# Row fetches of the last 128 tokens spread over selection, gates and U tail, and one row addition per V slab with eight landing buffers

## The reference, cut to what matters

```python
q = (xn @ wq)                      # 8 heads, two halves of 128 each
s = q . subkeys                    # 128 scores per half
v1, i1 = top_k(s[..., 0, :], 16); v2, i2 = top_k(s[..., 1, :], 16)
# the 16 best pairs of a head: idx in 0..16383, gate = softmax of their scores
h = einsum('md,med->me', x, u_tab[idx])          # 128 rows of U for each token
y = einsum('me,med->md', gate * gelu(h), v_tab[idx])
```

## Time and profile before

| | |
|---|---|
| median of 3 runs | 4130.0 us (4121.21 to 4146.6) |
| the profiled execution | 4155.08 us, span 4153.2 us |
| granted TensorE clock, mean | 0.918 |
| busy, share of the span | PE 88%, DVE 68%, ACT 35%, POOL 32% |
| moved by DMA | 814.18 MB, 196 GB/s over the span |

### The profile page before, as it was taken

The page is one execution under the profiler, slowest core; times in us unless marked ns, Lnnn a source line. Parts: engine busy times, 40 slices in busy tenths (PEclk is TensorE's granted clock), DMA queues, the critical chain, the costliest instruction groups (busy, mean ns, idle before and its releaser), DMA issues.

```text
span 4153.2 us, 60538 instructions
## 1 busy us (share of the span) xinstructions
PE 3668.9 (88%) x20002; PEld 3437.5 (83%) x20002; DVE 2809.7 (68%) x5900; ACT 1453.1 (35%) x2136; POOL 1335.5 (32%) x1052
## 2 busy tenths in 40 slices
PE   7966689999997998898899666899999979898987
PEld 5855579999997998898777555799999979888887
DVE  6244446889886787777562444478888868777774
ACT  4311123335674332233333111333357643332333
POOL 0000000214775446665000000011247744466650
PEclk9977779999998999999999676899999989999998
DMA  3200014446888999999321000144468889999991
GB/s 128 78 4 1 1 41 144 148 150 216 294 303 309 328 366 335 341 335 339 102 76 66 1 1 0 66 138 151 151 234 300 294 301 353 346 333 328 340 332 68
DMA packets 340506, 814.18 MB, mean 196 GB/s; under 512 B 25328, under 2 KB 189424, under 8 KB 336752
## 3 DMA queue, kind: packets, MB, share of 16 engines
q1 hardware_dynamic: 92592, 339.05, 23.0%
q0 software_dynamic: 73728, 268.47, 17.2%
q10 hardware_dynamic: 174016, 204.50, 14.8%
HBM read 709.16 MB, written 102.76 MB: 195 GB/s over the span
## 4 chain that ended last, share of the span: by engine, by line
PE 60%; DMA 18%; DVE 14%; issue 5%; DVEq 1%; POOL 1%; ACT 1%; ACTq 1%; SPq 0%; POOLq 0%; PEldq 0%
PE bank L368 15%; PE bank L369 14%; PE bank L370 14%; DMA gath<-slabs,rows_of 11%; PE bank L1100 4%; PE bank L938 3%; DMA g_sb<-gates_dram 3%; DMA gath<-u_rows,rows_of 2%; PE bank L391 1%; DVE acc L1656 1%; PE bank L415 1%; DVE wlo L365 1%; DVE act_w L1617 1%; DVE w_lo L1622 1%; PE bank L1020 1%
## 5 line engine op out<-in xcount | busy, mean ns | idle before, releaser
L365 DVE TENSOR_TENSOR wlo<-raw,whi 128x1024 fp32r<-128x1024 f32 x636 | 803.9, 1265 | 473.0 <-ACT whi L358 443.2
L368 PE MATMUL bank<-act_hi,whi 128*128 128x384 f32 (+1 forms) x3008 | 1082.4, 360 | 45.0 <-ACT hst L694 23.4
L369 PE MATMUL bank<-act_lo,whi 128*128 128x384 f32 (+1 forms) x3008 | 1068.3, 355 | 0.0
L370 PE MATMUL bank<-act_hi,wlo 128*128 128x384 f32 (+1 forms) x3008 | 1067.4, 355 | 0.0
L358 ACT ACTIVATE whi<-raw 128x1024 fp32r<-128x1024 f32 x636 | 673.7, 1060 | 522.9 <-PE bank L370 492.1
L368 PE MATMUL bank<-w_hi,whi 128*128 128x384 f32 x2048 | 713.4, 348 | 126.3 <-DVE w_lo L1622 126.0
L506 POOL TENSOR_TENSOR onehot<-onehot,cidx 128x800 f32<-128x800 f32 x56 | 123.9, 2243 | 1868.5 <-DVEq L1508 1868.5
L369 PE MATMUL bank<-w_lo,whi 128*128 128x384 f32 x2048 | 705.5, 344 | 0.0
L370 PE MATMUL bank<-w_hi,wlo 128*128 128x384 f32 x2048 | 704.5, 344 | 0.0
L368 PEld LDWEIGHTS bank<-act_hi,whi 128*128 128x128 f32 x3008 | 571.6, 190 | 92.7 <-ACT hst L694 24.1
L514 POOL DMA_INDIRECT gath<-slabs,rows_of x256 | 540.5, 2111 | 328.7 <-DVE acc L1656 277.6
(11 more groups left out here) (285 smaller groups left out, 3921.4 us busy)
## 6 DMA issues: line engine op xcount, KB each, us to landing
raw<-slabs SPq DMA_DIRECT2D x636, 512.0 KB, 3.7
hidden_dram<-hst ACTq DMA_DIRECT2D x256, 192.0 KB, 3.1
gates_dram<-stage ACTq DMA_DIRECT2D x24, 2048.0 KB, 7.5
h_sb<-hidden_dram ACTq DMA_DIRECT2D x64, 768.0 KB, 7.7
g_sb<-gates_dram ACTq DMA_DIRECT2D x64, 768.0 KB, 17.3
gath<-u_rows,rows_of POOLq DMA_INDIRECT x256, 7.3
gath<-slabs,rows_of POOLq DMA_INDIRECT x256, 8.7
res<-x_t SPq DMA_DIRECT2D x1, 2048.0 KB, 9.2
```

The source lines that it names most:

```text
L365: nc.vector.tensor_tensor(wlo[k][:], raw[k][:], whi[k][:].bitcast(F32), ALU.subtract).then_inc(s_slab_lo, 1)
L368: nc.tensor.matmul(out, a_hi, b_hi, start=first, stop=False)
L369: nc.tensor.matmul(out, a_hi, b_lo, start=False, stop=False)
L370: return nc.tensor.matmul(out, a_lo, b_hi, start=False, stop=last)
```

## The change

Row numbers of U are made head by head (in `sum_experts`), so that fetches can begin in selection. 32 dot products go into selection: five in each of heads 2 to 7, behind `split_lo` number 1, 3, 5, 7 and 8 of the head, and two after head 7. GpSimd issues five fetches after the `onehot` products of each of heads 1 to 6. 72 go into the gates, one in even batches and two in odd ones; 24 into the U tail, two per slab. V keeps one addition per slab, with eight buffers (four of them in memory that the U stage has freed). `x_nat` gets memory of its own and is made at the second slab of selection instead of near its end; the Gelu of the 128 tokens moves into the U tail; the first `load_hg` moves from slab 0 to slab 3 of the tail. Some constants (`dist`) are loaded again in each layer, to free memory. The diff, cut:

```diff
+GV = 8
+DOT_HEAD = 5
+DOT_SEL = 32
+DOT_LOOP = 12
+DOT_GATE = DOT_LOOP * N_BATCH // 8
+DOT_TAIL = P - DOT_SEL - DOT_GATE
+P_XNAT = 1
+X_TOK = 14
+DOT_AT = (1, 3, 5, 7, 8)
@@ SyncE
+                sp.dma_start(dist[:], consts_d[:, C_DIST:NCONST]).then_inc(S["dist_loaded"], 16)
@@ GpSimd
+                def gather(n):
+                    if n >= GR:
+                        pool.wait_ge(S["gath_used"], n - GR + 1)
+                    if n % TOPK == 0:
+                        pool.wait_ge(S["rows_ready"], n // TOPK + 1)
...
+                def gather_v(n):
+                    if n >= GV:
+                        pool.wait_ge(S["gath_used"], P + n - GV + 1)
+                    elif n >= GR:
+                        pool.wait_ge(s_used, S_V)
+                    else:
+                        pool.wait_ge(S["gath_used"], P - GR + n + 1)
...
                 for hd in range(PH - 1):
                     pool.wait_ge(S["places_ready"], hd + 1)
                     for t in range(NT):
                         rows = onehot[:, t * TOPK:(t + 1) * TOPK, :]
                         nc.gpsimd.tensor_tensor(rows, rows, cidx[:, t, :].unsqueeze(1).to_broadcast([P, TOPK, NC]),
                                                 ALU.mult).then_inc(S["picks_ready"], 1)
+                    if hd >= 1:
+                        for n in range(DOT_HEAD * (hd - 1), DOT_HEAD * hd):
+                            gather(n)
+                for n in range(DOT_HEAD * (PH - 2), DOT_SEL + GR - 1):
                     gather(n)
...
                     last.then_inc(S["hot1_ready"], 1)
-                    gather(b + GR - 1)
+                    for n in range(DOT_LOOP * b // 8, DOT_LOOP * (b + 1) // 8):
+                        gather(n + DOT_SEL + GR - 1)
@@ ScalarE, U tail
                     if x == 0:
+                        act.wait_ge(S["gm_ready"], 2 * TD // 8 + 4)
+                        act.dma_start(p_sb[:], p_t[layer]).then_inc(S["p_loaded"], 16)
+                    if x == 3:
                         act.wait_ge(S["stored_a"], TD // TG // 2 * 16 + 1)
                         act.wait_ge(S["stored_b"], TD // TG // 2 * 16 + 1)
...
                         load_hg(0, 0)
                         load_hg(1, 1)
...
+                    if x == X_TOK:
+                        act.wait_ge(S["gath_used"], P)
+                        nc.scalar.activation(w_tok, h_tok, ACT.Gelu).then_inc(S["tok_gelu"], 1)
@@ VectorE, selection
                 def sum_experts(hd):
                     step(V.tensor_reduce(expert[:, :, hd, :], picks, AX_X, ALU.add))
                     settle()
+                    V.tensor_scalar(rows_u[:, hd * TOPK:(hd + 1) * TOPK], expert[:, NTD, hd, :],
+                                    par[:, Q_ROWS:Q_ROWS + 1], None, ALU.add).then_inc(S["rows_ready"], 1)
...
                         for part in parts:
                             select(hd, part)
+                        if hd >= 2 and k in DOT_AT:
+                            if hd == 2 and k == DOT_AT[0]:
+                                dve.wait_ge(S["xnat_copied"], 2)
+                            n = DOT_HEAD * (hd - 2) + DOT_AT.index(k)
+                            dot(n, n % GR)
+                for n in range(DOT_HEAD * (PH - 2), DOT_SEL):
+                    dot(n, n % GR)
@@ VectorE, gates
-                        dot(q * 8 + b, b % GR)
+                        for c in range(DOT_LOOP * b // 8, DOT_LOOP * (b + 1) // 8):
+                            dot(q * DOT_LOOP + (DOT_SEL + c), c % GR)
@@ VectorE, V
                     for r in range(8):
-                        for c in range(per * r // 8, per * (r + 1) // 8):
-                            work(base + c, c % GR)
                         if not (final and r == 7):
                             split_lo(dve, it * 8 + (S_V + r + AHEAD), (S_V + r + AHEAD) % RING)
+                        add_row(it * 8 + r, r)
```

More of the change, by code:

```diff
@@ L86 @@
 REGION = 53200
[L88 to L93, removed]
+assert N_SLABS == S_WG + 8 and (S_WQ + P_GATE) % RING == 0
+C_ID, C_ONE, C_TRI, C_CHUNK, C_NEGT, C_POSD = [P * i for i in range(6)]
+C_IOTA = 6 * P
 C_POS = C_IOTA + P
 C_EPS = C_POS + NC
-NCONST = C_EPS + 2
+C_DIST = C_EPS + 2
+C_M16, C_M32, C_M64 = [C_DIST + T + P * i for i in range(3)]
+NCONST = C_DIST + T + 3 * P
 Q_MIX, Q_FFN, Q_PLE, Q_FIN = 0, 8, 16, 24
@@ L146, in trunk @@
         res = place("res", [P, KD, T], F32)
-        consts = place("consts", [P, NCONST], F32)
+        consts = place("consts", [P, C_DIST], F32)
         par = place("par", [P, NPAR], F32)
@@ L216, in trunk @@
         intra = place("intra", [P, H, P], F32, m3)
+        dist = place("dist", [P, T + 3 * P], F32, m3)
         vnew = u_sb
@@ L265, in trunk @@
         assert m[0] <= late
+        m = [after_e + KD * T * 4]
+        acc = [place(f"acc{i}", [P, KD, P], F32, m) for i in range(2)]
         m = [after_e]
@@ L272, in trunk @@
         gath = [place(f"gath{i}", [P, KD, P], F32, m) for i in range(GR)]
[L273 to L277, removed]
+        x_nat = place("x_nat", [P, KD, P], F32, m)
+        rows_u = place("rows_u", [P, P], I32, m)
+        h_tok = place("h_tok", [P, P], F32, m)[:]
         m = [act_base]
         hi_spare = place("hi_spare", [P, KD, T], F32, m)
-        lo_spare = place("lo_spare", [P, KD, T], F32, m)
-        h_tok = hi_spare[:, 7, TD:T]
+        gath_v = gath + [place(f"gath_v{i}", [P, KD, P], F32, m) for i in range(GV - GR)]
         w_tok = hi_spare[:, 6, TD:T]
-        x_nat = lo_spare[:, :, TD:T]
+        g_tok = hi_spare[:, 5, TD:T]
+        rows_v = hi_spare[:, 4, TD:T].bitcast(I32)
         bank = [ctx.enter_context(nc.psum_tensor(f"bank{i}", [P, T], F32)) for i in range(8)]
@@ L327, in trunk @@
         h_stored = [sem(f"h_stored{i}") for i in range(4)]
-        gath_loaded = [sem(f"gath_loaded{i}") for i in range(GR)]
+        gath_loaded = [sem(f"gath_loaded{i}") for i in range(GV)]
         per_layer = [S[n] for n in names] + slab_loaded + hg_loaded + h_stored
@@ L713, in _ @@
                         for c in range(2):
-                            nc.scalar.activation(x_nat[:, 4 * c:4 * c + 4, :], heads(4 + c), ACT.Copy
+                            nc.scalar.activation(x_nat[:, 4 * c:4 * c + 4, :], heads(6 + c), ACT.Copy
                                                  ).then_inc(S["xnat_copied"], 1)
@@ L827, in eight_values @@
                             load_hg(it * 2 + (2 + r // VB), r // VB)
[L828 to L832, removed]
+                with act.Fori(0, NKEYS // 8 - 1) as it:
                     eight_values(it, False)
@@ L1521, in sum_experts, with dot @@
                     settle()
+                    V.tensor_scalar(rows_u[:, hd * TOPK:(hd + 1) * TOPK], expert[:, NTD, hd, :],
+                                    par[:, Q_ROWS:Q_ROWS + 1], None, ALU.add).then_inc(S["rows_ready"], 1)
+                def dot(n, r):
+                    dve.wait_ge(gath_loaded[r], layer * (48 * 16) + n * 4 + (GR - r) * 4)
+                    col = h_tok[:, n:n + 1] if isinstance(n, int) else h_tok[:, bass.ds(n, 1)]
+                    V.scalar_tensor_tensor(gath[r][:], gath[r][:], 1.0, x_nat[:], ALU.mult, ALU.mult,
+                                           accum_out=col).then_inc(S["gath_used"], 1)
                 for p in range(4):
@@ L1587, in hot_rows @@
                     last.then_inc(S["hot2_ready"], 1)
-                def dot(n, r):
-                    dve.wait_ge(gath_loaded[r], layer * (N_GATH * 4) + n * 4 + (GR - r) * 4)
-                    col = h_tok[:, n:n + 1] if isinstance(n, int) else h_tok[:, bass.ds(n, 1)]
-                    V.scalar_tensor_tensor(gath[r][:], gath[r][:], 1.0, x_nat, ALU.mult, ALU.mult,
-                                           accum_out=col).then_inc(S["gath_used"], 1)
                 def eight_batches(q, final):
```

102 lines of the change are left out of this document (46 added, 56 removed).

## The result

The changed kernel takes 4211.2 us (median of 4, 4203.35 to 4215.71), the kernel before 4132.6 (4 runs): a ratio of 1.0187, with an interval of 1.015 to 1.0223. It is slower by 79 us. In eight profiled executions whose gates were the changed kernel's, the gates took 350 to 361 us a layer, and in eight whose V was the changed kernel's, V took 531 to 539, so a difference of a few us in these two stages tells nothing.

What follows compares the result with a forecast made beforehand. Selection and gates were taken as TensorE-bound, V as slowed by late rows and splits, the tail by two stalls. -154 - 32 + 66 + 134 = +14 on 4155.1 gave 4169, against the median 4145 us; range 4065 to 4240.

Steps and rivals of the forecast that it cites:

- the forecast's own: Whole kernel: the main forecast's range, 4085 to 4205 us, from the bounds of selection, U tail and V; chance 0.48.
- Slower by over 1%: Whole kernel: outcome over 4171 us, chance 0.38, from three slower rivals, less some, and a tenth of the forecast.
- the held-up fetch: Gates: rival that a fetch's issue takes 3.81 us as in V; 4236 us, slower by 2.6%; chance 0.15.
- a V bound by its loads: V: rival that g_sb's loads hold it at 4.5 us per slab; 4209 us; chance 0.15.
- buffers that don't help: V: rival that it stays at its pace because rows' way round doesn't bound it; 4299 us; chance 0.05.
- Part 4, gates: Odd gate batches: GpSimd's second fetch awaits VectorE's dot product ahead of due hot1 rows; 2.8 us per pair, 134 us loss.
- the gates hold their pace: Gates: rival that the 134 us loss falls away; 4011 us, faster by 2.9%; chance 0.17.
- Part 3, selection: Selection: added dot products and fetch waits exceed VectorE's idle time; 33 us a layer, 66 us loss.
- The six waits: Selection: VectorE waits for a fetch in each of six heads, 3.2 us each, 19 us a layer.
- Part 1, V: V: one row per slab and eight buffers give 4.25 us per slab, 544 us a layer; 154 us gain.
- Part 2, U tail: U tail: moving the store wait to slab 3 returns TensorE's 11.8 us and the clock behind it; 32 us gain.

Runs made afterwards that it cites:

- experiment 1: Changed kernel with GpSimd's fetches in the gates issued only behind the batch in which their buffer came free: 4117.7 us, ratio 0.998 to the kernel before.
- Experiment 2: Changed kernel with the gates' fetches reordered and one hot1 row of three moved from GpSimd to VectorE: 4064.0 us, ratio 0.984 to the kernel before.
- experiment 4: Changed kernel with three of a head's five fetches in selection issued ahead of the onehot products: 4177.4 us (one run).
- experiment 5: Changed kernel with selection's 32 dot products over 8 columns instead of 1024, fetches and waits kept: 4150.7 us (one run).
- experiment 10: Changed kernel with four landing buffers in V instead of eight, still one row addition per slab: 4207.1 us (one run).
- experiment 6: Changed kernel with the U tail's two load_hg at slabs 7 and 10, p's split at slab 3: 4216.4 us (one run).

## Why the prediction was right, and where it was off

The measured 4211 lies 66 us above the forecast of 4145: within the range for 8 in 10 (4065 to 4240), just outside the forecast's own (4085 to 4205). Of the 66, 34 are the sum's, +14 forecast and +48 found between the profiled executions; 25 were taken off for the place of the first profiled execution above its median, and the second lies 8 below its own. "Slower by over 1%" had 0.38, most of it for three rivals (the held-up fetch, a V bound by its loads, buffers that don't help), and in none of them did the kernel behave as described. What made it slower is the forecast's own mechanism, with the gain in the tail missing and a loss at V's end that the sum left out; that V gained 22 us more than forecast made up for a good part of this, by luck. Step by step:

**Part 4, gates: right in mechanism; the size agrees because two errors cancel.** 48 x 2.8 = 134 us was forecast, 138 measured, and experiment 1 shows the cause: with the order alone changed 96 of them go. The rival that the gates hold their pace falls with it. The chain of the prediction can be read in the changed kernel. VectorE, then GpSimd, then TensorE around one odd batch:

```profile
1181.80 1.23 DVE L372 TENSOR_TENSOR wlo<-raw,whi 128x1024 fp32r<-128x1024 f32 x1 [3.08 <-ACT whi L365]
...
1185.47 1.22 DVE L1557 SCALAR_TENSOR_TENSOR gath<-gath,x_nat 128x1024 f32<-128x1024 f32 x1
```

```profile
1186.97 1.68 POOL L516 DMA_INDIRECT gath<-u_rows,rows_u  x1 [3.00 <-DVE gath L1557]
1188.65 1.22 POOL L548 COPY n_cols<-selt 128x8 f32<-128x8 f32 x1
1189.95 0.66 POOL L551 TENSOR_TENSOR at_c<-consts 128x1 f32<-128x1 f32 x1
1190.59 1.87 POOL L553 TENSOR_SCALAR hot<-consts,n_cols 128x128 f32<-128x128 f32 x3
```

```profile
1192.59 0.59 PE L1127 MATMUL bank<-hot,hot 128*128 128x128 f32 x3 [2.78 <-POOL hot L553]
```

The dot product ends at 1186.69, the fetch that waits for it starts at 1186.97, and 5.49 us later the rows are done; 1.79 + 3.35 = 5.14 was worked out. TensorE stood still 2.78 us, with 2.8 forecast. But this is the longest kind of the 43 stalls; on the mean they are 2.2 us, 95 us in both layers and not 134. The rest is what the sum left out, the clock behind the stalls (0.93 and 0.95 in these windows). Experiment 2 shows its size, with the same matmuls and the same wait at the stage's start: TensorE is busy 275.4 us in each layer there, and 298.4 and 294.0 in the changed kernel. That is 42 us more for the same work, and 95 + 42 is the 137 us by which the two kernels' gates differ. Not foreseen was the second layer of the cause: GpSimd's own time bounds the gates when the order is mended (experiments 1 and 2).

By the Trainium skill (SBUF — State Buffer, "SBUF: two separate sides") GpSimd and VectorE lock a shared port pair for a whole instruction. The durations agree with it: in layer 0's gates of the changed kernel and of experiment 1, three rows took 1.78 to 1.87 us in the 38 cases in which they met no two-input operation of VectorE, and up to 4.44 where they met one. The rival that a fetch takes 3.81 us in the gates, as in V, did not come true; the fetches of layer 0's gates take 1.06 to 2.26 us, 1.68 at the median.

**Part 3, selection: right in mechanism, 5 us a layer too low.** 33 us forecast, 37.8 and 38.2 measured. The six waits were put at 3.2 us each and are 3.0; taking them away gives 17.5 us (experiment 4). That the work only costs once the idle time is used up is what experiment 5 shows. The missing 5 us are in the term of VectorE's work: its busy time in selection rose from 304.4 to 350.1 us, by 45.7, where 38.4 + 1.3 = 39.7 was counted. Five of the 32 dot products of a layer begin with GpSimd's `onehot` products and take 2.7 to 2.8 us instead of 1.22:

```profile
825.15 2.82 DVE L1557 SCALAR_TENSOR_TENSOR gath<-gath,x_nat 128x1024 f32<-128x1024 f32 x1
```

```profile
825.15 4.46 POOL L538 TENSOR_TENSOR onehot<-onehot,cidx 128x800 f32<-128x800 f32 x2 [27.63 <-DVEq L1536]
```

The place at the end of a head, chosen for the dot product, is where GpSimd starts.

**Part 1, V: right in mechanism, the size taken too small.** The term 4.25 us per slab for DMA's sake measured 4.17: the lower bound of the part. DMA moved 338 GB/s at share 0.96 and `g_sb` landed after 16.0 us at the median, under the 16.7 of the lead, so the rival of a V bound by its loads fell. But the eight buffers, to which the text gave a share of the gain, give nothing (experiment 10).

**Part 2, U tail: wrong in mechanism, though inside its bounds.** The step "the descriptors of four loads then lie under the two embedding slabs, which need no Gelu buffer" failed. These slabs need ScalarE all the same, to copy their results to `e_t`; and ScalarE was away longer than had been allowed for. Its queue in the changed kernel:

```profile
1415.78 5.55 ACTq L797 DMA_DIRECT2D h_sb<-hidden_dram  x1
1421.36 4.57 ACTq L799 DMA_DIRECT2D g_sb<-gates_dram  x1
1425.97 6.09 ACTq L714 DMA_DIRECT2D hidden_dram<-hst  x1
1432.16 0.49 ACT L721 ACTIVATE hst<-bank 128x384 f32<-128x384 f32 x1 [16.19 <-issue]
```

The trace of before had it already. Of ScalarE's 18.4 us of standing still, the wait for the gate store was only the first 7; from 1290.09 to 1301.20 it issued p's load, the same four loads and one store:

```profile
1290.09 0.36 ACTq L791 DMA_DIRECT2D p_sb<-p_t  x1
...
1292.18 3.85 ACTq L770 DMA_DIRECT2D h_sb<-hidden_dram  x1
1296.06 1.77 ACTq L772 DMA_DIRECT2D g_sb<-gates_dram  x1
1297.87 3.33 ACTq L687 DMA_DIRECT2D hidden_dram<-hst  x1
1301.30 0.49 ACT L694 ACTIVATE hst<-bank 128x384 f32<-128x384 f32 x1 [18.36 <-issue]
```

The prediction put all of TensorE's 11.8 us down to the store. Moving the loads took the store out of the wait and carried the issues to where TensorE needs ScalarE again. TensorE's waits in the tail of layer 0 add up to 25.2 us in the changed kernel, against 23.3 before: 4 us gained where 32 were forecast, and not by less waiting.

**V's end: not in the sum.** 15 us. The prediction followed the row additions to the last slab and not to the one instruction behind them, for which TensorE waits; before, the additions and their sum were done ahead of the last eight slabs. With this term and the tail at its measured value the sum would have been 14 + 15 + 28 = +57, against 48 between the two profiled executions.

## What to carry to other kernels

When work is spread into a stage with spare time, ask not only how busy each engine is there, but what stands behind each new wait on the engine that makes it: here one fetch, ahead of three rows that were due, cost more than half of what V won. A wait that goes may have been hiding something else (a queue's issues, a sum at the end); say what lies beneath it before counting it as gain. A second bound shows itself only once the first is mended, so measure the repairs alone and together; and leave each part of a change out by itself, for one of them, here the eight buffers, may give nothing. When a forecast comes out right, compare its terms too: a stall taken too long and a clock left out can add up to the measured number.

## What the runs showed of the hardware

An issue on ScalarE's queue, 0.34 to 0.48 us at the median, took 5.55, 4.57 and 6.09 us in a row behind a first pair of loads of hidden values and gates, and 10.66 us in experiment 6 behind one pair; the engine did nothing meanwhile that stood behind it. GpSimd's copy of 128x8 took 0.20 us or 1.22, its three rows of 128x128 between 1.78 and 4.44 us. VectorE's dot product, 1.22 us alone, took 2.82 when it began together with GpSimd's product of 128x800. A fetch took 1.06 us to issue when it began in a gap of VectorE, and 1.8 at the median when it began in a two-input operation (10 and 50 of the fetches in the changed kernel's gates, layer 0). With DMA at 338 GB/s and share 0.96, TensorE still ran V without one wait worth naming.
